# Inverting the diagonal blocks of a chunked delta scan per unit instead of per pair of units

## What is computed

```
lmat  = where(tril_strict, einsum('bnhid,bnhjd->bnhij', k_beta, k) * decay, 0)
t_inv = triangular_solve(eye + lmat, eye, lower=True, unit_diagonal=True)
u     = t_inv @ v_beta
w     = t_inv @ (k_beta * exp(g))
v_new = u_i - w_i @ state
o_i   = (q_i * exp(g_i)) @ state + a_intra @ v_new
state = state * exp(g_last) + (k_i * exp(g_last - g_i))^T @ v_new
```

## Time and profile before

| | us |
|---|---|
| median of 3 runs | 2997.08 (2994.06 to 3004.97) |
| profiled execution | 2997.56 |
| its span | 2995.8 |
| first matmul of unit 0's levels to the end of the scan's last state update | 629.03 to 1286.57 |
| PE busy over the span | 2695.3 (90%) |
| DVE busy over the span | 1351.4 (45%) |

### The profile page before, as it was taken

How to read it: one execution, slowest core, us unless ns; L and a number is a source line. 1 busy time by engine, 2 the same in 40 slices (tenths; PEclk the granted TensorE clock), 3 DMA queues, 4 the chain that set the end, 5 groups by cost and what they waited for, 6 DMA issues and landing times. The chain is left out here.

```text
span 2995.8 us, 45883 instructions
## 1 busy us (share of the span) xinstructions
PE 2695.3 (90%) x18134; PEld 2545.7 (85%) x18134; DVE 1351.4 (45%) x2151; ACT 1037.7 (35%) x1791; POOL 597.5 (20%) x488
## 2 busy tenths in 40 slices
PE   7999999979788889836999868989999999999999
PEld 3898999878778888834777768889999999999999
DVE  4564332246445556545889843352222243222222
ACT  4222332334323343235778742332222222222211
POOL 1001223333334333132333222110111000111100
PEclk9999999979769899958999979999999999999999
DMA  5324664443344343140000035332222232222232
GB/s 200 142 79 129 218 218 164 145 125 97 101 133 111 92 130 89 55 169 25 17 17 16 8 122 214 102 115 71 77 70 77 84 107 92 77 70 77 69 95 69
DMA packets 197241, 304.68 MB, mean 102 GB/s; under 512 B 80560, under 2 KB 122064, under 8 KB 195536
## 3 DMA queue, kind: packets, MB, share of 16 engines
q1 hardware_dynamic: 194192, 286.63, 30.2%
q10 hardware_dynamic: 2880, 15.73, 1.5%
HBM read 238.77 MB, written 63.52 MB: 101 GB/s over the span
## 5 line engine op out<-in xcount | busy, mean ns | idle before, releaser
L277 PE MATMUL f_ps<-mf_h_hi,mf_w_hi 128*128 128x320 f32 x1408 | 435.1, 309 | 1.4 <-PEq L2015 1.4
L277 PE MATMUL f_ps<-mf_h_lo,mf_w_hi 128*128 128x320 f32 x1408 | 435.1, 309 | 0.0
L277 PE MATMUL f_ps<-mf_h_hi,mf_w_lo 128*128 128x320 f32 x1408 | 435.1, 309 | 0.0
L2448 DVE TENSOR_TENSOR mf_w_lo<-mf_w_raw,mf_w_hi 128x1024 fp32r<-128x1024 f32 (+1 forms) x135 | 188.9, 1399 | 431.6 <-ACT mf_w_hi L2300 431.3
L277 PE MATMUL proj_ps<-h_hi,w_hi 128*128 128x320 f32 x896 | 282.9, 316 | 6.0 <-DVE w_lo L571 5.6
L277 PE MATMUL proj_ps<-h_lo,w_hi 128*128 128x320 f32 x896 | 278.2, 310 | 0.0
L277 PE MATMUL proj_ps<-h_hi,w_lo 128*128 128x320 f32 x896 | 278.0, 310 | 0.0
L277 PEld LDWEIGHTS f_ps<-mf_h_hi,mf_w_hi 128*128 128x128 f32 x1408 | 264.3, 188 | 1.6 <-issue 1.6
L277 PEld LDWEIGHTS f_ps<-mf_h_lo,mf_w_hi 128*128 128x128 f32 x1408 | 264.3, 188 | 0.0
L277 PEld LDWEIGHTS f_ps<-mf_h_hi,mf_w_lo 128*128 128x128 f32 x1408 | 264.3, 188 | 0.0
L277 PE MATMUL f_ps<-f_ff_hi,mf_w_hi 128*128 128x320 f32 x704 | 220.0, 313 | 6.9 <-POOL f_ff_lo L2374 6.9
(11 more groups left out here) (330 smaller groups left out, 6407.1 us busy)
## 6 DMA issues: line engine op xcount, KB each, us to landing
mf_w_raw<-w_up_dram SPq DMA_DIRECT2D x88, 512.0 KB, 3.5
w_raw<-w_in_dram SPq DMA_DIRECT2D x48, 512.0 KB, 4.7
w_ada_raw<-w_ada_dram SPq DMA_DIRECT2D x16, 1024.0 KB, 5.0
mf_w_raw<-w_mix_dram SPq DMA_DIRECT2D x32, 512.0 KB, 4.7
mf_w_raw<-w_down_dram SPq DMA_DIRECT2D x32, 448.0 KB, 3.3
delta_t<-delta_tile ACTq DMA_DIRECT2D x10, 1024.0 KB, 6.7
decay_t<-g_rows SPq DMA_DIRECT2D x40, 256.0 KB, 5.3
kq_t<-delta_t SPq DMA_DIRECT2D x20, 512.0 KB, 4.4
```

The source lines that it names most:

```text
L277: ins = nc.tensor.matmul(out, w(k), a(k), start=(first and n == 0 and q == 0), stop=(last and n == len(ks) - 1 and q == 2))
L2448: nc.vector.tensor_tensor(wlo[:, slot, 0:nk], raw[:, slot, 0:nk], whi[:, slot, 0:nk].bitcast(F32), ALU.subtract).then_inc(E[half]["lo"], 1)
```

## The change

Each unit's blocks are inverted alone, on 64 partitions, by `diagonal(k)`. Direction is handled by strides (`si, sj`) instead of a turned copy, so `turn_backward` goes. All steps are placed by unit: `blocks_out(k)` and `blocks_in(k)` in body k-3, `diagonal(k)` in body k-2, `inverse_pair(k)`, `inverse_out(k)` and `inverse_in(k)` in body k-1. `diagonal(k)` is in four pieces: rows 1 to 5 in the second level, rows 6 and 7 in the third, step 8 after the refinement's y_res, step 9 after w_t.

```
-        BASE_AT = {LV[0]: (1, 2, 3, 4, 5), LV[1]: (6, 7, 8), LV[2]: (9,)}
+        BASE_AT = {LV[1]: (1, 2, 3, 4, 5), LV[2]: (6, 7), "r": (8,), "x": (9,)}
...
-            def blocks_in(j):
-                if j:
-                    sp.wait_ge(e["base_step"], BASE * j)
-                sp.wait_ge(e["blocks_out"], 256 * (j + 1))
-                for d, to in ((0, dg), (1, db)):
-                    sp.dma_start(to[64 * d:64 * d + 64], io["diag"][d].rearrange("b h j i -> (b h) (j i)")).then_inc(e["blocks_in"], 16)
...
+            def blocks_in(k):
+                if k:
+                    sp.wait_ge(e["base_step"], BASE * k)
+                sp.wait_ge(e["blocks_out"], 128 * (k + 1))
+                sp.dma_start(dg[:], io["diag"][k % 2].rearrange("b h j i -> (b h) (j i)")).then_inc(e["blocks_in"], 16)
+
+            def inverse_out(k):
+                sp.wait_ge(e["xo_ready"], 2 * k + 2)
+                if k >= 2:
+                    sp.wait_ge(e["xb_in"], 128 * (k - 1))
+                for x in range(2):
+                    dst = io["diag_inv"][k % 2, :, x].rearrange("b h i j -> b h (i j)")
+                    sp.dma_start(dst, xo[:, x].bitcast(F32)).then_inc(e["pair_out"], 16)
...
-                if has(u + 1) and u % 2 == 0:
+                if has(u + 1):
+                    if u == -1:
+                        sp.wait_ge(e["xb_zero"], 1)
+                    inverse_out(u + 1)
                     inverse_in(u + 1)
...
-                if has(u + 1) and u % 2:
-                    inverse_out((u + 1) // 2)
-                    if u == -1:
-                        sp.wait_ge(e["xb_zero"], 1)
-                    inverse_in(u + 1)
+                if has(u + AHEAD):
+                    blocks_out(u + AHEAD)
...
-                if has(u + AHEAD) and (u + AHEAD) % 2:
-                    blocks_in((u + AHEAD) // 2)
+                if has(u + AHEAD):
+                    blocks_in(u + AHEAD)
...
-                if has(u + 1) and u % 2:
-                    turn_backward((u + 1) // 2)
...
-                    if has(u + 1) and u % 2 and lv == LV[2]:
-                        inverse_pair((u + 1) // 2)
+                    if has(u + 1) and lv == LV[0]:
+                        inverse_pair(u + 1)
...
-                    if has(u + 1) and u % 2:
-                        diagonal((u + 1) // 2, BASE_AT[lv])
+                    if has(u + 2) and lv in BASE_AT:
+                        diagonal(u + 2, BASE_AT[lv])
...
+                if has(u + 2):
+                    diagonal(u + 2, BASE_AT["r"])
...
+                if has(u + 2):
+                    diagonal(u + 2, BASE_AT["x"])
```

More of the change, by code:

```diff
@@ L765, in delta_scan @@
         XB = sb("x_base", [P, 2, NH, P], F32R)
[L766 to L770, removed]
+        dg = sb("diag_blocks", [NH * 8, 256])
+        xc = sb("diag_inverse", [NH * 8, 256])
+        dt_, dsum = sb("diag_products", [NH * 8, 512]), sb("diag_sums", [NH * 8, 64])
+        xo = sb("diag_inverse_pair", [NH * 8, 2, 256], F32R)
         XX = sb("x_inv", [P, 2, 2, H4, P], F32R)
@@ L784, in delta_scan @@
         FB = ctx.enter_context(nc.psum_tensor("bank_F", [P, 512], F32))
-        names = ("eyes_ready zeroed state_in kept exp_ready relu_ready di_ready ds_ready nb_ready ni_ready xb_zero blocks_out blocks_in turned_in base_init base_step xo_ready pair_out xb_in "
+        names = ("eyes_ready zeroed state_in kept exp_ready relu_ready di_ready ds_ready nb_ready ni_ready xb_zero blocks_out blocks_in base_init base_step xo_ready pair_out xb_in "
                  "a_ps a_out z_ps x_ready xr_ps w_ready "
@@ L886, in blocks_out @@
                 if k >= 2:
-                    sp.wait_ge(e["blocks_in"], 32 * (k // 2))
+                    sp.wait_ge(e["blocks_in"], 16 * (k - 1))
                 sp.wait_ge(e["a_out"], a_index["k", k, 1, 1] + 1)
@@ L891, in blocks_out @@
                     sp.dma_start(io["diag"][k % 2, b].rearrange("h j i -> j h i"), NTf[rows, k % RING].rearrange("p c h i -> p (c h) i")[:, :, rows]).then_inc(e["blocks_out"], 16)
-            def blocks_in(j):
-                if j:
-                    sp.wait_ge(e["base_step"], BASE * j)
-                sp.wait_ge(e["blocks_out"], 256 * (j + 1))
-                for d, to in ((0, dg), (1, db)):
-                    sp.dma_start(to[64 * d:64 * d + 64], io["diag"][d].rearrange("b h j i -> (b h) (j i)")).then_inc(e["blocks_in"], 16)
[L900 to L907, removed]
+            def blocks_in(k):
[10 more added lines that the diff above has]
+                    sp.dma_start(dst, xo[:, x].bitcast(F32)).then_inc(e["pair_out"], 16)
             def inverse_in(k):
-                sp.wait_ge(e["pair_out"], 64 * (k // 2 + 1))
+                sp.wait_ge(e["pair_out"], 32 * (k + 1))
                 if k:
@@ L989, in _ @@
                     load_again(u + 1)
-                if has(u + AHEAD):
-                    blocks_out(u + AHEAD)
                 if has(u + AHEAD + 2) and u + AHEAD >= 0:
@@ L1080, in decay, with inverse_pair @@
                 nc.scalar.activation(DT[:, u % 2, c], DT[:, u % 2, c], ACT.Exp, scale=-1.0).then_inc(e["exp_ready"], 1)
[L1082 to L1093, removed]
+            def inverse_pair(k):
+                act.wait_ge(e["base_step"], BASE * (k + 1))
+                if k:
+                    act.wait_ge(e["pair_out"], 32 * k)
+                as_is = xc[:]
+                turned = xc[:].rearrange("p (i j) -> p j i", i=16)
+                for x in range(2):
+                    nc.scalar.activation(xo[:, x] if x == k % 2 else xo[:, x].rearrange("p (i j) -> p i j", i=16), as_is if x == k % 2 else turned, ACT.Copy).then_inc(e["xo_ready"], 1)
             def body(u):
-                if has(u + 1) and u % 2:
-                    turn_backward((u + 1) // 2)
                 for i, lv in enumerate(LV):
@@ L1164, in view, with diagonal @@
                 return bass.AP(tensor=a.tensor, offset=a.offset + offset, ap=[list(a.ap[0])] + [list(d) for d in dims])
-            def diagonal(j, rows):
+            def diagonal(k, rows):
                 d, x = dg[:], xc[:]
-                si, sj = 1, 16
-                at = [BASE * j + STEP_AT[rows[0]]]
+                si, sj = (1, 16) if k % 2 == 0 else (16, 1)
+                at = [BASE * k + STEP_AT[rows[0]]]
                 def step(ins):
@@ L1177, in diagonal @@
                 if rows[0] == 1:
-                    dve.wait_ge(e["blocks_in"], 32 * (j + 1))
-                    dve.wait_ge(e["turned_in"], j + 1)
+                    dve.wait_ge(e["blocks_in"], 16 * (k + 1))
                     dve.wait_ge(e["base_init"], 2)
-                    if j:
-                        dve.wait_ge(e["xo_ready"], 2 * j)
+                    if k:
+                        dve.wait_ge(e["xo_ready"], 2 * k)
                 for i in rows:
```

## The result

The changed kernel takes 3091.74 us in the median of 4 runs (3082.29 to 3100.56). The kernel before took 3000.02 beside it (median of 4, 2994.06 to 3004.97). The ratio is 1.031, with a 95% interval of 1.027 to 1.034: slower by 3%. The forecast of 3016 us had the sign and most of the mechanism, but the time lies outside its range of 2928 to 3060.

The account below looks back on a forecast made before the run. PE, busy 90% of the span, was taken as bound by its work, its waits and the clock lost after them. Added 54 us (waits and others) plus 86 (clock falls) less 121 removed gave +19: 3016 us, eight-in-ten range 2928 to 3060.

Parts of the forecast that it names:

- items 1 and 2: PE's x_base waits at the end of odd units (38.3 us) and turn_backward's holds (15 us) go.
- item 3: PE's 11.14 us wait for unit 0 goes and the prologue's VectorE queue is relieved: 12 us taken.
- item 4: Clock lost behind the removed waits, in even units and units 0, 1, 5, 6 and 11, comes back: 56 us.
- Steps 8 and 9 don't hide: At each unit boundary VectorE's queue makes PE wait 2.3 us more; 42 us over eighteen bodies.
- A half as wide block inversion is no cheaper: On VectorE each of 20 units, on 64 partitions, pays what a pair of units paid.
- the slow rival: VectorE late twice: POOL holds up rows 1 to 5, third level waits 1.8 us more; 3093 us, chance 0.15.
- The falls of the clock: After the 1.9 us wait before the z product the clock falls at 11 of 18 boundaries, 7.8 us each: 86 us.
- those on the fast side: Clock comes back early (2955 us, 0.17), clock does not fall (2931, 0.10), steps 8 and 9 hide (2882, 0.06).
- VectorE is late twice in a unit: Third level also waits 1.8 us more and the clock falls in nearly every unit; 3093 us, chance 0.15.
- Steps 8 and 9 hide too: PE reaches the boundary later than reckoned, only some 5 us of the added remain; about 2882 us, chance 0.06.

Follow-up runs that it names:

- freed: Kernel spread with ScalarE's inverse_pair copy moved ahead of the x_inv copies of the second level; 2908.40 us, ratio 0.970.
- pad1: Kernel freed with one more product like step 8's (64x512, never read) on VectorE behind each unit's w_t; 2933.59 us, ratio 0.979.
- spread: Changed kernel with step 8 in the third level of body k-2, step 9 and inverse_pair in body k-1's first and second levels; 2971.36 us, ratio 0.992.
- only9: Changed kernel with step 8 moved into the third level, only step 9 left at the boundary; 2972.22 us, ratio 0.992.
- cover: Changed kernel with six more independent projection matmuls ahead of each unit's first z product, none in two later slots; 3011.86 us, ratio 1.006.
- padb: Kernel freed with two unread products, 64x512 and 64x256, on VectorE behind each unit's w_t; 3045.47 us, ratio 1.019.
- pad2: Kernel freed with two unread 64x512 products on VectorE behind each unit's w_t; 3077.74 us, ratio 1.026.

## Why the prediction was wrong

**What the change takes away: the waits.** Right. Kernel freed has the change's scheme without its late steps, so its scan shows this part alone: TensorE is idle 31.9 us (584.43 less 552.57) against 82.9, 51 less, with 38 and 15 forecast for items 1 and 2, 53 together.

**The start (item 3)** gave 8.2 us for 12. Unit 0 begins at 620.81 instead of 629.03, but it still waits for x_base, whose transfers SyncE issues from 615.18 (SyncE's and TensorE's timelines, changed kernel):

```profile
615.18 3.95 SPq L912 DMA_DIRECT2D x_base<-diag_inv  x8
```

```profile
620.81 0.45 PE L1228 MATMUL bank_A<-x_base,n_t_eye 128*128 128x128 f32 x1 [6.09 <-DMA x_base<-diag_inv]
```

**The clock lost behind these waits (item 4)** is the first step that failed: 56 us were booked, and TensorE's busy time falls by only 22 (574.69 to 552.57 in freed). I had put the low clock of units 5 and 6 down to the turn_backward wait, 19 us, from the rows' 31.05 and 31.16 busy. In freed these units have under 1 us of idle time each and are still at 0.60, with 33.3 us busy: 4.4 us more in the two together, not 19 less. And unit 0, booked at 6.5 us less, is busy 33.44 for 26.79, 6.7 more. A low clock after a wait need not be due to it. In pad1, unit 5 has a wait of 1.36 us before its first z product and is busy less, 27.29 us at 0.77. Why these two units, the ones without projection matmuls, run low with hardly a wait stays open; no run changed them alone.

**Steps 8 and 9 don't hide.** Right in place and about right in size: 2.9 us of wait at a boundary for 2.3. "A half as wide block inversion is no cheaper" held: a product of 512 elements took 1.04 us on 64 partitions in freed and 1.05 on 128 before. What was missed is that it is dearer in its new place. The groups of step 8's products in the changed kernel, then in freed:

```profile
L1178 DVE TENSOR_TENSOR diag_products<-diag_blocks,diag_inverse 64x512 f32<-64x512 f32 x20 | 33.7, 1683 | 0.0
```

```profile
L1178 DVE TENSOR_TENSOR diag_products<-diag_blocks,diag_inverse 64x512 f32<-64x512 f32 x20 | 20.8, 1038 | 0.7
```

Beside GpSimd's masks at the end of a unit it takes 1.90 us (964.17 above), away from them 1.04. GpSimd's own instruction is held up as well, for it takes 2.11 us where the one of its kind just before takes 1.28 (its timeline, changed kernel):

```profile
962.77 1.28 POOL L1044 TENSOR_TENSOR n_t<-decay_t,offdiag_sb 128x512 f32<-128x512 f32 x1
...
965.12 2.11 POOL L1044 TENSOR_TENSOR n_t<-decay_t,offdiag_sb 128x512 f32<-128x512 f32 x1
```

Over all 13 traces, 153 products of this kind on 64 partitions had no such GpSimd instruction beside them and took 1.02 to 1.08 us; 164 had one for over half of their time and took 1.70 in the median, at most 2.17. The page GPSIMD Engine Reference of the Trainium skill, section Specifications, says that GpSimd shares its SBUF interfaces with VectorE, with contention for VectorE instructions of two SBUF inputs, and the traces agree. I had read it for rows 1 to 5 in the slow rival, where nothing of the kind happened, and not for step 8.

**The falls of the clock** are the second step that failed, and the larger. The forecast was "11 of 18" at 7.8 us, 86 us. The change's scan has 147 us more of busy TensorE than freed's, with falls at all 18. But units 5, 6 and 7 run low in freed too (33.33, 33.27 and 33.74 busy), and the change adds only 2 us in the three together. The other 15 units share 146 us, 9.7 each: unit 9 lost 8.2 and unit 10 11.3 (34.18 and 37.22 for 25.95), and the range is 7.8 to 13.7. So both the count and the price were too low: four falls more at 7.8 are 31 of the 61 us missed here, and the rest is that a fall in this place cost 9.7 and not 7.8. On the count, I weighed two falls after 1.29 and 1.78 us against a feeling that it "will not always come together with as little other work". The table above is what was wanted: after 1.5 to 2.0 us it fell 28 times of 34. The two falls were thin evidence all the same: the wait of 1.78 us stands in the changed kernel too (1.76 us, at 572.12), and there no fall follows. The page TensorE: Matmul & The Clock Gate of the Trainium skill, section "Why this matters for your kernels", warns only of idle gaps longer than these. The traces disagree: 28 of the 34 waits of 1.5 to 2.0 us before the z product were followed by a fall, though only 1 of 37 under 1.25 us. The measured rows decide.

**The sum.** Against the 3016 forecast: 34 for item 4 (56 less 22), 61 for the falls (147 less 86), 4 for the start, and waits 15 us shorter than booked (forecast 54 added less 53 removed, so 1 more; measured 37 added, from freed to the change, and 51 removed, so 13.7 less). 3016 + 34 + 61 + 4 - 15 = 3100; the profiled execution took 3100.56.

**The rivals.** None of those on the fast side came true. "VectorE is late twice in a unit" gave the nearest time, 3093, but for another reason: no second wait appears in the third level, and the falls come behind the boundary's waits alone. "Steps 8 and 9 hide too" is what freed builds, at 2908 for the 2882 given there; item 4 and the start are the difference. Whether inverting pairs of units at the same distance ahead would do as well was not tried.

## What to carry to other kernels

Look at the engine that a shared queue makes late before placing work at a hand-over: a few microseconds of VectorE between two stages of TensorE cost 3 us of waiting and 8 to 14 us of clock in a unit, and some microseconds earlier or later the same instructions cost next to nothing. Where traces show the clock falling after waits as long as the one you forecast, and in the same place, count the fall as often as they show it; in another place the same wait can be harmless more often than not (spread). And before a low clock is booked as the price of a wait, look for a unit of the same kind without the wait.

## What the runs showed of the hardware

- Between a wait of 1.13 us and one of 1.71 before the same matmul unit 9's time goes from 27 to 30 us to 34 to 38 (only9, pad1 and cover; padb and pad2). After 0.94 and 1.13 us, 2.4 us apart (cover, unit 9), the clock stayed at 1.00.
- After a fall in the changed kernel the clock stays at 0.50 for 17 to 34 us with TensorE busy nearly throughout, and not as long each time for the same wait: 17 us in unit 9 (1.93 us) and 24 in unit 10 (1.95). In padb it is 14 or 20 us behind 1.71, and in spread 3 to 7 behind a third level's wait of 1.5 to 1.8.
- Step 8's product, of two SBUF inputs, takes 1.02 to 1.08 us on VectorE with no GpSimd instruction of its kind beside it, and 1.70 in the median, at most 2.17, beside one. Halving its partitions from 128 to 64 doesn't shorten it (1.05 and 1.04 us).
